# Hybrid gMLP and mixture-of-experts layer: expert 0's rows gathered and transposed in one step, and the router's group picked by max and max_index

## What is computed

```python
g_prob = jax.nn.softmax(xt @ w_group + b_group, axis=-1)
g_w, g_idx = lax.top_k(g_prob, 1)                     # the best of 4 groups
e_logits = (xt @ w_exp + b_exp).reshape(T, 4, 8)
e_logits = jnp.take_along_axis(e_logits, g_idx[:, :, None], axis=1)[:, 0]
e_w, e_idx = lax.top_k(jax.nn.softmax(e_logits, axis=-1), 2)
e_w = e_w / jnp.sum(e_w, axis=-1, keepdims=True)
...
# for each expert e, on the rows xb that chose it:
y = (silu(xb @ w_gate[e]) * (xb @ w_up[e])) @ w_down[e]   # 2048 -> 512 -> 2048
out[rows] += weight * y
```

## Time and profile before

| | |
|---|---|
| median of 3 runs | 1217.09 us (1214.74 to 1217.89) |
| the profiled execution | 1217.03 us, of which its span is 1214.9 us |
| PE busy | 894.1 us, 74% of the span |
| PEld busy | 507.3 us, 42% |
| DVE busy | 374.9 us, 31% |
| ACT busy | 222.7 us, 18% |
| HBM read | 459.09 MB, 380 GB/s over the span |

### The profile page before, as it was taken

How to read it: one execution, slowest core, us unless ns; L and a number is a source line. 1 busy time by engine, 2 the same in 40 slices (tenths; PEclk the granted TensorE clock), 3 DMA queues, 4 the chain that set the end, 5 groups by cost and what they waited for, 6 DMA issues and landing times.

```text
span 1214.9 us, 17531 instructions
## 1 busy us (share of the span) xinstructions
PE 894.1 (74%) x7815; PEld 507.3 (42%) x7815; DVE 374.9 (31%) x473; ACT 222.7 (18%) x388; POOL 20.1 (2%) x54
## 2 busy tenths in 40 slices
PE   9999999999985556666666666666666656666785
PEld 7788888887432222222222222222222222222332
DVE  5454846445232222222222222222222222222232
ACT  6544555434100000000000000000000000000002
POOL 1100000000200000000000000000000000000000
PEclk9999999999997777777877878787878788777878
DMA  8876557857899999999999999999999999999995
GB/s 286 324 274 237 194 220 262 296 169 286 365 426 429 430 431 432 433 430 433 432 434 429 433 430 434 432 432 432 431 432 432 432 431 432 432 432 432 423 425 228
DMA packets 45956, 461.70 MB, mean 380 GB/s; under 512 B 3768, under 2 KB 4384, under 8 KB 30560
## 3 DMA queue, kind: packets, MB, share of 16 engines
q1 hardware_dynamic: 45184, 458.24, 90.6%
q0 software_dynamic: 656, 2.94, 0.7%
q10 hardware_dynamic: 80, 0.02, 0.0%
HBM read 459.09 MB, written 2.10 MB: 380 GB/s over the span
## 4 chain that ended last, share of the span: by engine, by line
PE 48%; DMA 47%; ACT 1%; DVE 1%; SPq 1%; issue 1%; POOLq 0%; POOL 0%; DVEq 0%; ACTq 0%
DMA low_slots<-in_e_w_up 47%; PE scattered_out L1207 21%; PE bank L1407 13%; PE bank L1443 5%; PE pair L1369 3%; PE scattered_out L1456 2%; PE pair L1378 1%; ACT arena L673 1%; DMA w_raw<-in_a_w_in 1%; SPq L372 0%; PE bank L1308 0%; DVE w_lo L794 0%; SPq L388 0%; PE pair L1460 0%; PE scattered_out L1460 0%
## 5 line engine op out<-in xcount | busy, mean ns | idle before, releaser
L1044 DVE TENSOR_TENSOR acc<-scattered_out,acc 128x2048 f32<-128x2048 f32 x60 | 137.5, 2292 | 627.3 <-PE scattered_out L1456 627.3
L1407 PE MATMUL bank<-low_slots,arena 128*32 128x256 f32 x2048 | 153.8, 456 | 146.4 <-DMA low_slots<-in_e_w_up 145.7
L1407 PE MATMUL bank<-high_slots,arena 128*32 128x256 f32 x1952 | 142.1, 452 | 140.5 <-DMA high_slots<-in_e_w_up 140.5
L1407 PEld LDWEIGHTS bank<-low_slots,arena 128*32 128x32 f32 x2048 | 83.2, 127 | 217.2 <-issue 185.7
L1407 PEld LDWEIGHTS bank<-high_slots,arena 128*32 128x32 f32 x1952 | 77.6, 126 | 210.8 <-issue 180.6
L794 DVE TENSOR_TENSOR w_lo<-w_raw,w_hi 128x1024 fp32r<-128x1024 f32 x95 | 117.0, 1232 | 121.9 <-ACT w_hi L512 121.5
L512 ACT CAST w_hi<-w_raw 128x1024 fp32r<-128x1024 f32 x95 | 99.8, 1051 | 132.5 <-PE scattered_out L1207 132.2
L1207 PE MATMUL scattered_out<-w_hi,xT_first 128*128 128x512 f32 x376 | 122.0, 396 | 0.4 <-DVE w_lo L794 0.3
L1207 PE MATMUL scattered_out<-w_hi,xT_second 128*128 128x512 f32 x376 | 122.1, 396 | 0.1
L683 ACT COPY arena<-bank 128x256 f32<-128x256 f32 x32 | 11.9, 372 | 573.2 <-PE bank L1407 573.2
L1443 PE MATMUL bank<-down_slots,arena 128*32 128x512 f32 x944 | 107.9, 595 | 0.7 <-DVE arena L1038 0.7
(11 more groups left out here) (225 smaller groups left out, 497.3 us busy)
## 6 DMA issues: line engine op xcount, KB each, us to landing
down_slots<-in_e_w_down SPq DMA_DIRECT2D x26, 4096.0 KB, 21.1
low_slots<-in_e_w_gate SPq DMA_DIRECT2D x13, 4096.0 KB, 30.6
low_slots<-in_e_w_up SPq DMA_DIRECT2D x13, 4096.0 KB, 39.8
high_slots<-in_e_w_gate SPq DMA_DIRECT2D x13, 4096.0 KB, 30.4
high_slots<-in_e_w_up SPq DMA_DIRECT2D x13, 4096.0 KB, 39.6
w_raw<-in_a_w_in SPq DMA_DIRECT2D x64, 512.0 KB, 3.6
w_raw<-in_a_w_out SPq DMA_DIRECT2D x32, 512.0 KB, 4.7
low_slots<-in_e_w_up SPq DMA_DIRECT2D x6, 2048.0 KB, 21.1
```

Source lines behind the costliest of these rows:

```text
L1044: dve.tensor_tensor(acc[:, t, :], OUT[:, :], (acc if e else h)[:, t, :], ALU.add).then_inc(acc_done, 1)
L1407: ins = pe.matmul(GU[c * CAP:(c + 1) * CAP, 0:256], xeT[:, k % KC, 2 * a + k // KC, :], gate_columns(tiles[c // 2][:, k, :], c % 2), start ...
```

## The change

For expert 0 alone, `gather`, `copy_xe` and `transpose_xe` are replaced by `gather_first`: for each of the 16 k and both t, a matmul with 128 columns of `h` (every 16th, starting at k) as the stationary side and `sel` (32 columns) as the moving one. Its result is already transposed. It is done in pieces, four k, then two, two and eight, and the pieces stand between the gate-up steps of expert 0's first half. DVE scales each group when it is there (`scale_first`, 128, 128 and 256 elements for each partition). The results go to three PSUM banks. The semaphore `gu_quarter` becomes `gu_pair`, counted after two and after four k, and SP loads chunks 11 and 12 in three pieces each (2, 2 and 4 of 8 parts). `xe` and `xeT` change places in SBUF, so that `xeT` can be written while the router's small tiles are still in use. In the router the group logits stand behind the expert logits, padded to 8 columns; `max` and `max_index` find the group, and one comparison with a table of group numbers (`group_e`) and one multiply-add mask the rest.

```diff
-        xe = part(0, 512)
-        xeT = part(512, 1024, "p (k j c) -> p k j c", k=KC, j=NQ)
+        xeT = part(0, 512, "p (k j c) -> p k j c", k=KC, j=NQ)
+        xe = part(512, 1024)
...
+        XT_FIRST, XT_NEXT = bank[0], bank[1]
...
-            sp.wait_ge(gu_quarter, 1)
-            for i in (IN_ACC + 2, IN_ACC + 3):
-                half = 1 if i % NCH >= 4 else 4
-                sp.dma_start(chunk_tile(i)[:, 0:half, :], expert_chunk(i)[:, 0:half, :]
-                             ).then_inc(first_part[i - IN_ACC - 2], 16)
+            for n in range(2):
+                sp.wait_ge(gu_pair, n + 1)
+                for i in (IN_ACC + 2, IN_ACC + 3):
+                    load_piece(i, 2 * n, 2 * n + 2, first_part[i - IN_ACC - 2])
             sp.wait_ge(gu_half, 1)
             for i in (IN_ACC + 2, IN_ACC + 3):
+                load_piece(i, 4, 8, chunk_in[chunk_at(i)[0]])
...
-            then_step(dve.tensor_reduce(g_max, lg_g, AX_X, ALU.max))
-            first_of(group_hot, lg_g, g_max, NGRP, g_scratch)
-            then_step(dve.tensor_scalar(group_hot, group_hot, BIG, -BIG, ALU.mult, ALU.add))
-            then_step(dve.tensor_tensor(masked.rearrange("p a (g e) -> p a g e", g=NGRP),
+            for t in range(NT):
+                dve.max(g_top[:, t, :], lg_pad[:, t, :]).then_inc(r_step, 1)
+            for t in range(NT):
+                dve.wait_ge(r_step, steps[0] + t + 1)
+                dve.max_index(top_at[:, 0, t, :], g_top[:, t, :], lg_pad[:, t, :]).then_inc(r_step, 1)
+            steps[0] += 2 * NT
+            dve.wait_ge(r_step, steps[0])
+            then_step(dve.tensor_tensor(off, group_e[:, :, :], top_at[:, 0, :, 0:1].to_broadcast([P, NT, NEXP]),
+                                        ALU.not_equal))
+            then_step(dve.scalar_tensor_tensor(out=masked, in0=off, scalar=-BIG, in1=lg_e, op0=ALU.mult, op1=ALU.add))
...
+            def scale_first(ready, src, lo, hi, done):
+                dve.wait_ge(ready, 1)
+                dve.tensor_tensor(xeT[:, :, lo:hi, :], src[:, 0:(hi - lo) * KC * CAP].rearrange("p (j b c) -> p b j c", b=KC, c=CAP),
+                                  g_of[:, :, lo:hi, :], ALU.mult).then_inc(done, 1)
...
+            dve.wait_ge(g_rows_in, 16)
+            scale_first(xT_first_ps, XT_FIRST, 0, 1, xeT_first)
+            scale_first(xT_next_ps, XT_NEXT, 1, 2, xeT_next)
             choose(0)
-            dve.wait_ge(g_rows_in, 16)
-            scale_xeT(0)
+            scale_first(xe_ps, TRX, 2, NQ, xeT_ready)
             choose(1)
...
+            def gather_first(lo, hi):
+                for t in range(NT):
+                    pe.wait_ge((sel_first, sel_ready)[t], 1)
+                    for k in range(lo, hi):
+                        at = k if k < KC else k - KC if k < 2 * KC else k - 2 * KC
+                        ins = pe.matmul((XT_FIRST, XT_NEXT, TRX, TRX)[k // KC][:, at * CAP:(at + 1) * CAP],
+                                        h[:, t, :].rearrange("q (p k) -> q k p", k=KD)[:, k, :], sel[:, 0, t, :],
+                                        start=(t == 0 and k in (0, KC, 2 * KC)), stop=(t == NT - 1), skip_group_check=True)
+                return ins
...
+            def first_expert():
+                gather_first(0, 4).then_inc(xT_first_ps, 1)
+                gather_first(4, 6)
+                wait_chunk(0)
+                wait_chunk(1)
+                tiles = [chunk_tile(0), chunk_tile(1)]
+                pe.wait_ge(xeT_first, 1)
+                gate_up_of(0, 0, tiles, 0, 2).then_inc(gu_pair, 1)
+                gather_first(6, 8).then_inc(xT_next_ps, 1)
+                gate_up_of(0, 0, tiles, 2, 4).then_inc(gu_pair, 1)
+                pe.wait_ge(xeT_next, 1)
+                gate_up_of(0, 0, tiles, 4, 8).then_inc(gu_half, 1)
+                gather_first(8, KD).then_inc(xe_ps, 1)
+                transpose_scat(0)
+                gate_up_half(0, 1)
+                gather(1)
+                transpose_gu(0)
+                transpose_xe(1)
+                down(0)
```

More of the change, by code:

```diff
@@ L123, in hybrid_layer @@
         rstd_h, rms_h, ssq_h, rstd_o, rms_o, ssq_o = (rows[:, i, :] for i in range(5, 11))
-        (g_max, g_sum, d21, e21, w1, w2, column) = (rc[:, i, :] for i in range(7))
-        group_hot, g_shifted, g_exp, g_scratch = (rt[:, i, :, 0:NGRP] for i in range(4))
+        (g_sum, d21, e21, w1, w2) = (rc[:, i, :] for i in range(5))
+        g_top = rt[:, 0, :, 0:8]
+        g_shifted, g_exp = (rt[:, i, :, 0:NGRP] for i in (1, 2))
         masked, masked2, hot1, hot2, off = (rt[:, i, :, :] for i in range(4, 9))
@@ L936, in then_step @@
                 dve.wait_ge(r_step, steps[0])
[L938 to L949, removed]
             then_step(dve.reciprocal(rstd_h, rms_h))
-            then_step(dve.memset(top[:, :, :], 0.0))
+            dve.wait_ge(tops_ready, 2)
             dve.wait_ge(consts, ALL_CONSTS)
@@ L1359, in gather @@
             def gather(e, m=0):
[L1360 to L1364, removed]
+                pe.wait_ge(sel_ready, 2 * m + (e + 1))
+                pe.wait_ge(scatT_ready, 2 * m + e)
                 for t in range(NT):
-                    if e == 0 and t == 1:
-                        pe.wait_ge(sel_ready, 1)
                     for j in range(NB):
@@ L1373, in transpose_xe @@
             def transpose_xe(e, m=0):
[L1374 to L1376 removed]
+                pe.wait_ge(xe_ready, 2 * m + e)
+                pe.wait_ge(xeT_ready, 2 * m + e)
                 for b in range(KC):
@@ L1384, in transpose_xe, with gate_up_of @@
                 ins.then_inc(scat_ps, 1)
+            def gather_first(lo, hi):
[7 more added lines that the diff above has]
+                return ins
+            def gate_up_of(e, a, tiles, lo, hi):
+                for k in range(lo, hi):
+                    for c in range(NQ):
+                        ins = pe.matmul(GU[c * CAP:(c + 1) * CAP, 0:256], xeT[:, k % KC, 2 * a + k // KC, :],
+                                        gate_columns(tiles[c // 2][:, k, :], c % 2),
+                                        start=(a == 0 and k == 0), stop=(a == 1 and k == 7))
+                return ins
+            def first_expert():
[17 more added lines that the diff above has]
+                down(0)
             def wait_chunk(i):
@@ L1404, in gate_up_half @@
                     wait_chunk(NCH * e + 2 * a + 1)
[L1405 to L1412, removed]
+                gate_up_of(e, a, tiles, 0, 8).then_inc((gu_half, gu_ps)[a], 1)
             def gate_up(e, m=0):
@@ L1491, in expert @@
                 gate_up(e, m)
-                if e > 0:
-                    scatter(e - 1, 0, m)
+                scatter(e - 1, 0, m)
                 gather(e + 1, m)
@@ L1587, in _ @@
             pe.sem_inc(x_used, 1)
-            gather(0)
-            transpose_xe(0)
-            for e in range(BREAK):
+            first_expert()
+            for e in range(1, BREAK):
                 expert(e)
```

59 lines of the change are left out of this document (34 added, 25 removed).

## The result

| | median | runs |
|---|---|---|
| before | 1216.37 us | 1214.74 to 1217.89, 4 runs |
| after | 1228.37 us | 1224.0 to 1229.38, 4 runs |

The ratio is 1.0087, with a 95% interval of 1.0072 to 1.0102: 12 us slower in the medians, where 1.2 us faster was forecast. The profiled execution took 1224.0 us, with a span of 1221.8 us.

A forecast was written before the change was run, and what follows sets the result against it. Transfers of expert weights bound the kernel, so only DMA idle time after the mixer counts. Of 2.85 us won at the first hole, 1.6 go into a second: 1217.03 - 1.2 = 1215.8 us, range 1213.0 to 1219.0.

The forecast's parts named there:

- the hole: DMA nearly idle from 306 to 313 us, behind the mixer: 4.7 us lost, the most that filling it can win.
- only the bytes set the end: From 313 us on, PE's savings or losses cost nothing so long as the DMA queue never runs empty.
- The router: The new group pick saves 0.25 us, so the first gather starts at 303.40 and not 303.65.
- The gather's price: 32 float32 matmuls of gather_first for expert 0 at 0.214 us each, 6.8 us of PE in all.
- the second rival: Strided weight loads run at half speed: 0.43 us a gather matmul, 1222.7 us; chance 0.08.
- The bound of 0.28: Upper bound for a gather matmul: two loads at the transposes' pace of 0.14 us.
- half speed: Strided weight loads in gather_first make a matmul 0.43 us, chunk 13 flows from 326.9, 1222.7 us; chance 0.08.
- The sum: Expert 0's order: first issue 2.85 us earlier, 1.6 us of it lost again at chunk 13, 1.2 us won.
- the second hole: A new DMA gap of 1.6 us before chunk 13, whose issue moves from 315.53 to 318.58.
- the cover of 5.7 us: Before, chunk 13 was issued 5.7 us before the transfers ahead of it ended; the change uses this up.
- The pieces of 0.5 MB: The small first transfers of chunks 11 and 12 were taken to reach 427 GB/s, like 1 MB pieces.
- The rule of 1 MiB: Transfers should be 1 MiB or more; applied to the small pieces it loses about 1.3 us, leaving near nothing.

The follow-up runs named there:

- the ladders: Kernel before plus unused matmuls or transposes, columns 4 to 64 bytes apart, ahead of expert 1's gate and up; once each: 1220.3, 1237.9, 1217.5 us.
- both causes removed: Changed kernel with adjacent stationary columns and 128 moving columns (the identity) for 32, expert 0's rows not gathered: 1214.53 us against 1217.11, 0.9986.
- the adjacent one: Changed kernel with gather_first taking 128 adjacent columns of h instead of every 16th, 32 moving columns kept: 1217.24 us against 1216.56, 1.0018.

## Why the prediction was wrong

- **What bounds the kernel, and the hole: right up to the last two experts.** What the transfers lacked between 306 and 334, 9.8 us, is there at expert 30 as 10.0 us. From 360 to 1100 the rate is 431 to 432 GB/s as before, and no later expert ran the queue empty. But "only the bytes set the end" does not hold for the last 58 us of before, where 3.1 of the 10 us were given back.
- **The router: right within its size.** From the end of the scaled logits to the first `max` over the experts lay 300.46 - 298.97 = 1.49 us before and 300.53 - 299.37 = 1.16 us after, 0.33 us less; the forecast was 0.25.
- **The gather's price: wrong, and this step decided.** "The stride that is there costs nothing, so I take 0.214." It was 0.45 us for a matmul, beyond the 0.25 at which the forecast called itself wrong. It had held L1378 against the second rival; the ladders showed that transposes are free of a cost which a float32 matmul pays in full from 16 bytes on. The bound of 0.28 came from the same transposes and fell with it. The rival "half speed" named the mechanism, 0.43 us a matmul and 1222.7 us, and had got a chance of 0.08. With the clock at 1.00, as that rival tacitly assumed, the chip gave 1222.4. Even adjacent columns cost more than 0.214: 3.71 / 16 = 0.23 us for a matmul, and 0.24 with 128 moving columns (32 in 7.81 us).
- **The clock: missing.** The sum took 0.465 us per k at a clock of 1.00 throughout, since every row from 300 to 365 read 1.00. No step asked what `gather_first` does to it: 32 moving columns for each 128 loaded. It cost 2.9 to 3.5 us on the way to chunk 13's issue, and 2.7 us in the spans of the profiles (1219.6 to 1222.3). In the medians it is about 5 us (1222.4 to 1227.6), with some of the open 3 to 5 us in it. That the first issue came 3.6 us later than forecast, counted from the gather, is 2.8 us by the loads and 0.9 by the clock, less 0.2 in the step to SP.
- **The order and the second hole: right in kind, a little small in size.** With both causes removed 16.1 us lay between the first gather and chunk 13's issue, where 15.2 was forecast; the 0.9 us are the gather's 7.81 us against 6.85. The second hole is there in every kernel with this order (321 to 324 in the adjacent one; 295 and 229 GB/s from 321 to 323 with 128 moving columns). So the cover of 5.7 us in the earlier trace rows was used up, as the forecast said. Of the gain little is left: 0.2 us in the transfers, beside the router's 0.3. That this kernel's time was 0.9986 of before, and the forecast 0.999, is luck in part: in the profiles its span is 2.6 us shorter, and all of that lies behind expert 30's landing (55.4 us to the end in place of 58.4).
- **The pieces of 0.5 MB: right.** They moved 397 to 433 GB/s. The rule of 1 MiB that the forecast took from the Trainium skill ("DMA: Bandwidth & Descriptors", "Measured") did not show at 4 KB a partition. Where a first piece had 2 KB a partition the rate did fall, to 287 GB/s.

## What to carry to other kernels

Take the price of a matmul's stationary side from a row of a matmul, with the same distance between columns, and not from a transpose; if no such row is there, the two prices of these runs, 0.11 us a load up to 8 bytes and 0.22 from 16 on, are the bounds. Before a stream of matmuls with few moving columns is put into a stretch at the full clock, price what stands behind it at half the clock too. And when a transfer is issued earlier by making PE do more behind it, look at the next issue as well: what had been cover there is spent.

## What the runs showed of the hardware

- A float32 load of 128 stationary columns takes 0.11 us with columns 4 or 8 bytes apart, 0.17 us at 12, 0.22 us at 16 and 0.20 to 0.23 at 64 (3.27 us for 16, 7.20 us for 32), at a granted clock of 1.00. At 0.50 adjacent columns take 0.23 us (8 in 1.85 us) and those 64 bytes apart 0.23 (8 in 1.87 us), so the distance costs nothing more there.
- A float32 transpose takes 0.11 to 0.12 us at 4, 16 and 64 bytes alike, at 1.00.
- Behind a stream of gather matmuls with 32 moving columns for each 128 loaded the granted clock stood at 0.50 in three profiles; with 128 moving columns, at the same pace, it stayed at 1.00 in two.
- Chunks of 2 MB cut so that each partition gets 4, 4 and 8 KB moved at 397 to 433 GB/s; cut into 2, 4 and 10 KB they moved at 287 to 318 GB/s, with the engines busy at a share of 0.93 to 0.98.
